# The opening of a two-block transformer kernel, with the first modulation made in two halves

## The chip, the cores and the metric

The kernel runs on one core of one Trainium2 chip. The metric is the device time of one execution in microseconds (us). The engines are TensorE (PE in the profile, its weight loads are PEld), VectorE (DVE), ScalarE (ACT), GpSimd (POOL) and SyncE (SP), which here only issues DMAs.

## The reference

Two blocks run one after the other on 256 tokens of width 1024, all in float32. The part that the opening computes is this:

```
cs  = silu(c)
mod = (cs @ ada_w[l] + ada_b[l]).reshape(3 sub-layers, [shift, scale, gate], 1024)
h   = rmsnorm(x, norm_g[l, 0]) * (1 + mod[0, scale]) + mod[0, shift]
x   = x + 0.5 * mod[0, gate] * (silu(h @ w_gate) * (h @ w_up)) @ w_down
...
(the same for a mixer of attention and convolution, and for a second FFN; two such layers;
 then a second block: FFN, a mixer of attention and a gated linear recurrence, FFN)
```

Before the first product with a weight of the FFN can start, `cs @ ada_w` must be known for the shift and the scale: two times 1024 columns of a matrix with 1024 rows, 8 MB in all.

## The kernel before

**Stages.** The program has nine stages (FFN, mixer, FFN, FFN, mixer, FFN, then FFN, mixer 2, FFN). Each reads its weights in units of 1 MB (128 partitions x 2048). SyncE loads a unit into one of three slots of `raw`, ScalarE rounds it to float32r into `hi` (`split`), VectorE subtracts to get the rest in `lo` (`split`, or `low_part` for half of a unit), and TensorE multiplies three times (`tok3`, `mm3`: high by low, low by high, high by high). The semaphores are `raw_full` (landed), `hi_done`, `lo_done` and `unit_done`. Unit n+3 takes the slot of unit n once its low part is made. Every engine works through its own instruction list strictly in the order in which the code is written; nothing is scheduled at run time, and semaphores alone tie the lists together.

**Tiles and chunks.** The 256 tokens are two tiles of 128. The 1024 columns of `x` are eight chunks of 128, which are turned by TensorE (`turn_x`) into PSUM (`PC`), scaled and shifted into `ub_b` and split into `nh` (high) and `nl` (low, by `lows`). ScalarE and VectorE do this in `apply`, pair of chunks by pair of chunks; `nh_done` and `nl_done` count the pairs.

**The opening.** The 8 MB of the first modulation come as eight units of 256 columns. Units 0 to 3 are the shift of chunks 0 to 7 (two chunks each), units 4 to 7 are the scale. VectorE makes five of them (0, 2, 4, 5, 7; `ada_unit`: one multiplication and seven multiply-adds over 128 x 256), and TensorE then sums each over the partitions with two products by a column of ones. TensorE makes the other three itself (`ada_cols_of`: 16 products of one column, each with a new weight of 128 x 128). Both write columns of `MOD` in PSUM. When all 16 columns are there (`mod_done`), `mods(0)` on VectorE makes `modt` (shift) and `nsc` (scale times gain), and `mods_rdy` lets `apply(0, 0)` start.

**The first FFN.** Its `up` products read two weight units: unit 0 holds the rows of chunks 0 to 3, unit 1 those of chunks 4 to 7 (`up(i, kh, t)`: group i, half kh, tile t; 12 products of 512 columns in `wide`). Group 0 is `up(0,0,0)`, `up(0,1,0)`, `up(0,0,1)`, `up(0,1,1)`. Then come the products of `bias_lines` and group 1.

**Two other places.** In the mixer of the first block twelve units make q and k (`unit_both`); VectorE adds their two halves (`qk_done`, one per unit), and `tick` starts the attention of one head and tile: logits on TensorE into the bank `SC`, bias and maximum on VectorE (`lg_done`), exponential on ScalarE. In the mixer of the second block `lru(3, 3)` makes the low part `cL` of the last two chunks of the recurrence, for which the product `yc` 0 waits at its chunk 6 (`first_recurrent`).

## Time and profile before

| | us |
|---|---|
| median of 3 runs | 2093.26 (2092.66 to 2093.48) |
| the profiled execution | 2095.6 |
| its span, first to last instruction | 2093.5 |
| PE busy in it | 2059.9 (98%) |
| DVE busy | 1432.5 (68%) |
| ACT busy | 1028.6 (49%) |
| DMA, mean over the span | 209 GB/s |

The profiled execution's own time is 2.1 us above its span, and 2.3 us above the median of the runs shown.

### The profile page before, as it was taken

The numbers are of one execution on the slowest core, as the hardware profiler recorded it, in microseconds if no ns is written. First come the engines' busy times: TensorE is split into PE (matmuls) and PEld (weight loads), VectorE is DVE, ScalarE is ACT, GpSimd is POOL, SyncE is SP. The second block draws the span as 40 slices with busy tenths as digits, with TensorE's granted clock in tenths as the row PEclk, the third lists the DMA queues.
The fourth block names the chain that finished last, engine by engine and source line by source line (L and its number), as shares of the span: only waits on it lengthen the run. The fifth ranks groups of instructions, "written<-read, shape, count | busy, mean of one in ns | idle before, by whom it ended". The sixth has DMA issues, their size and how long they took to land.

```text
span 2093.5 us, 28979 instructions
## 1 busy us (share of the span) xinstructions
PE 2059.9 (98%) x11649; PEld 1790.4 (86%) x11649; DVE 1432.5 (68%) x1822; ACT 1028.6 (49%) x1279; POOL 36.3 (2%) x78
## 2 busy tenths in 40 slices
PE   7999999999999999999999999999999999999998
PEld 7788888999888888888899998888788799998887
DVE  5887788668777677767866786455654669656454
ACT  4443544444554363445444445444644668646443
POOL 0000000000000000000000000000000010000000
PEclk9999999999999999999999999999999999999999
DMA  9787698447678748868865496654755454456652
GB/s 316 258 283 251 193 290 253 128 139 253 230 256 267 245 168 277 264 202 260 287 183 145 143 300 192 203 188 141 234 188 183 135 160 137 161 183 210 192 190 80
DMA packets 355929, 438.04 MB, mean 209 GB/s; under 512 B 9571, under 2 KB 323371, under 8 KB 355796
## 3 DMA queue, kind: packets, MB, share of 16 engines
q1 hardware_dynamic: 350592, 420.51, 61.7%
q0 software_dynamic: 4160, 14.23, 3.1%
q8 instruction: 92, 1.51, 0.3%
q10 hardware_dynamic: 1044, 1.46, 0.2%
q14 instruction: 41, 0.34, 0.0%
HBM read 435.05 MB, written 1.11 MB: 208 GB/s over the span
## 4 chain that ended last, share of the span: by engine, by line
PE 88%; DVE 5%; ACT 4%; issue 1%; DMA 1%; DVEq 1%; SPq 0%; ACTq 0%
PE PC L1808 7%; PE PC L1810 7%; PE PC L1809 7%; PE PA L1808 6%; PE PA L1810 6%; PE PA L1809 6%; PE PB L1808 6%; PE PB L1810 6%; PE PB L1809 6%; PE PA L1801 4%; PE PA L1802 4%; PE PA L1803 4%; PE PC L1839 3%; PE PC L1976 2%; PE PC L1801 2%; PE PC L1803 2%
## 5 line engine op out<-in xcount | busy, mean ns | idle before, releaser
L1172 DVE TENSOR_TENSOR lo<-raw,hi 128x2048 fp32r<-128x2048 f32 x274 | 626.7, 2289 | 209.5 <-ACT hi L696 208.4
L696 ACT ACTIVATE hi<-raw 128x2048 fp32r<-128x2048 f32 x277 | 529.3, 1912 | 260.1 <-PE PC L1810 114.8
L1198 DVE SCALAR_TENSOR_TENSOR acc<-raw,cs,acc 128x256 f32<-128x256 f32 x448 | 217.2, 485 | 34.4 <-issue 0.9
L1808 PE MATMUL PA<-hi,nn 128*128 128x512 f32 (+1 forms) x528 | 210.3, 398 | 7.0 <-DVE nn L1274 5.9
L1801 PE MATMUL PA<-nn,hi 128*128 128x256 f32 x720 | 209.0, 290 | 0.4 <-ACT f L1089 0.4
L1810 PE MATMUL PA<-hi,nn 128*128 128x512 f32 (+1 forms) x528 | 206.0, 390 | 0.0
L1809 PE MATMUL PA<-lo,nn 128*128 128x512 f32 (+1 forms) x528 | 205.5, 389 | 0.0
L1802 PE MATMUL PA<-nn,lo 128*128 128x256 f32 x720 | 203.6, 283 | 0.0
L1803 PE MATMUL PA<-nn,hi 128*128 128x256 f32 x720 | 203.6, 283 | 0.0
L1808 PE MATMUL PB<-hi,nn 128*128 128x512 f32 x400 | 158.2, 395 | 0.5 <-DVE nn L1274 0.5
L1810 PE MATMUL PB<-hi,nn 128*128 128x512 f32 x400 | 156.6, 391 | 0.0
L1809 PE MATMUL PB<-lo,nn 128*128 128x512 f32 x400 | 156.2, 391 | 0.0
L1172 DVE TENSOR_TENSOR w<-raw,w 128x2048 fp32r<-128x2048 f32 x51 | 116.8, 2289 | 50.4 <-ACT w L696 50.4
L1808 PE MATMUL PC<-hi,cL 128*128 128x512 f32 x384 | 151.1, 393 | 0.0
L1810 PE MATMUL PC<-hi,cH 128*128 128x512 f32 x384 | 149.6, 390 | 0.0
L1809 PE MATMUL PC<-lo,cH 128*128 128x512 f32 x384 | 149.5, 389 | 0.0
L1801 PEld LDWEIGHTS PA<-nn,hi 128*128 128x128 f32 x720 | 137.9, 192 | 1.9 <-issue 0.6
L1802 PEld LDWEIGHTS PA<-nn,lo 128*128 128x128 f32 x720 | 137.9, 192 | 0.1
L1803 PEld LDWEIGHTS PA<-nn,hi 128*128 128x128 f32 x720 | 137.8, 191 | 0.0
L1808 PEld LDWEIGHTS PA<-hi,nn 128*128 128x128 f32 x528 | 100.7, 191 | 30.4 <-issue 9.1
L696 ACT ACTIVATE w<-raw 128x2048 fp32r<-128x2048 f32 x51 | 97.5, 1911 | 48.0 <-PE PC L1810 44.1
L1810 PEld LDWEIGHTS PA<-hi,nn 128*128 128x128 f32 x528 | 100.6, 190 | 20.9
(317 smaller groups left out, 4088.8 us busy)
## 6 DMA issues: line engine op xcount, KB each, us to landing
raw<-in_w_in SPq DMA_DIRECT2D x90, 1024.0 KB, 5.4
raw<-in_ada_w SPq DMA_DIRECT2D x66, 1024.0 KB, 7.4
raw<-in_ffn_w_gate SPq DMA_DIRECT2D x88, 512.0 KB, 4.1
raw<-in_ffn_w_up SPq DMA_DIRECT2D x88, 512.0 KB, 5.2
raw<-in_ffn_w_down SPq DMA_DIRECT2D x44, 1024.0 KB, 5.2
raw<-in_ffn_w SPq DMA_DIRECT2D x88, 512.0 KB, 4.8
raw<-in_ffn_w SPq DMA_DIRECT2D x22, 1024.0 KB, 4.8
raw<-in_w_o SPq DMA_DIRECT2D x12, 1024.0 KB, 6.6
```

What stands on the lines that cost most here:

```text
L696: A(parts_of(n)[0], raw[:, n % 3, :], ACT.Copy).then_inc(hi_done, 1)
L1172: V.tensor_tensor(l, raw[:, n % 3, :], h.bitcast(F32), ALU.subtract).then_inc(lo_done, 1)
L1198: i = V.scalar_tensor_tensor(o, w[:, k, :], cs[:, k:k + 1], o, ALU.mult, ALU.add)
L1801: MM(o, wh[:, c0:c0 + w], xl, start=first, stop=False, skip_group_check=True)
L1802: MM(o, wl[:, c0:c0 + w], xh, start=False, stop=False, skip_group_check=True)
L1803: return MM(o, wh[:, c0:c0 + w], xh, start=False, stop=last, skip_group_check=True)
L1808: MM(o, xl, wh[:, c0:c0 + w], start=first, stop=False, skip_group_check=True)
L1809: MM(o, xh, wl[:, c0:c0 + w], start=False, stop=False, skip_group_check=True)
L1810: return MM(o, xh, wh[:, c0:c0 + w], start=False, stop=last, skip_group_check=True)
L1839: MM(o[:, m * 512:(m + 1) * 512].rearrange("p (e t) -> p e t", e=2), wh[:, c], nn[:, :, kk, :], start=kk == 0, stop=False, skip_group_chec ...
L1976: i = MM(SC[:, c0:c0 + w], qt[p0:p0 + HD, qc, (s % 2) * P:(s % 2 + 1) * P], kt[p0:p0 + HD, kc, 0:w], start=True, stop=True, skip_group_che ...
```

## The change

1. The eight units of the modulation are loaded in the order 0, 4, 1, 5, 2, 6, 3, 7: shift and scale of chunks 0 to 3 come first. The list of who makes which place stays (places 0, 2, 4, 5, 7 by VectorE, places 1, 3, 6 by TensorE). The FFN's weight unit 0 is loaded after the sixth place instead of after the eighth.
2. `mods(0)` becomes `half_mods(0)` and `half_mods(1)`, each for four chunks, with the semaphores `mod_first` and `half_rdy` for the first. ScalarE scales and shifts chunks 0 to 3 of both tiles, splits weight units 0 and 1 in between, and then does chunks 4 to 7 of both tiles; VectorE no longer scales any of tile 1.
3. TensorE's sums over partitions stand in a function of their own (`ada_sums(n)`, for the n-th of VectorE's places; it signals `mod_first` after the second and `mod_done` after the fifth). TensorE multiplies unit 0 with tile 0, then makes place 6 (`ada_cols_of(6)`), multiplies unit 0 with tile 1, sums the last unit, and then multiplies unit 1 with both tiles.
4. In the two mixers of the first block the first `tick` waits for 11 of the 12 additions of q and k, and the second for all 12.
5. In the second block's mixer VectorE does `lru(3, 3)` before `split(b + 19)` instead of after it.

```diff
+FIRST_ADA = (0, 4, 1, 5, 2, 6, 3, 7)
+def place(Aq, t, j):
+    if Aq == 0:
+        return 4 * (j // 2) + 2 * t + j % 2 + 1
+    return Aq * 8 + t * 4 + j + 1
...
@@ SyncE
-            for u in range(8):
-                sp.dma_start(first_ada(u), ada_v[0][:, :, u * UC:(u + 1) * UC])                    .then_inc(raw_full[u] if u < 4 else ada_in[u - 4], 16)
+            for u, c in enumerate(FIRST_ADA):
+                if u == 6:
+                    load(0, wg_v[0][:, 0:4, 0:UC], wu_v[0][:, 0:4, 0:UC])
+                sp.dma_start(first_ada(u), ada_v[0][:, :, c * UC:(c + 1) * UC])\
+                    .then_inc(raw_full[u] if u < 4 else ada_in[u - 4], 16)
...
@@ ScalarE
+            def first_apply(t, h):
+                act.wait_ge(tn_done, 2 * t + h + 1)
+                if t:
+                    act.wait_ge(nl_done, 4 * h + 2)
+                else:
+                    act.wait_ge(mods_rdy if h else half_rdy, 1)
+                for j in (2 * h, 2 * h + 1):
+                    for c in (2 * j, 2 * j + 1):
+                        i = A(ub_b[:, c, :], PC[:, t * D + c * P:t * D + (c + 1) * P], ACT.Identity,
+                              scale=nsc[:, c:c + 1], bias=modt[:, c:c + 1])
+                    i.then_inc(ua_done, 1)
+                    act.wait_ge(ua_done, place(0, t, j))
+                    A(nh[:, 2 * j:2 * j + 2, t * P:(t + 1) * P], ub_b[:, 2 * j:2 * j + 2, :], ACT.Copy)\
+                        .then_inc(nh_done, 1)
+            first_apply(0, 0)
             split(0)
-            apply(0, 0, lambda: split(1))
-            apply(0, 1)
+            first_apply(1, 0)
+            split(1)
+            first_apply(0, 1)
+            first_apply(1, 1)
...
@@ VectorE
+            def half_mods(h, done):
+                c = slice(4 * h, 4 * h + 4)
+                V.tensor_tensor(modt[:, :].rearrange("p (a k) -> p a k", a=2)[:, :, c],
+                                MOD.rearrange("p (a k) -> p a k", a=2)[:, :, c],
+                                vec[:, 0:16].rearrange("p (a k) -> p a k", a=2)[:, :, c], ALU.add)
+                dve.drain()
+                V.scalar_tensor_tensor(nsc[:, c], modt[:, 8 + 4 * h:12 + 4 * h], 1.0,
+                                       vec[:, V_NORM + 4 * h:V_NORM + 4 * h + 4], ALU.add, ALU.mult).then_inc(done, 1)
+                dve.drain()
...
                 if n == 3:
                     normed(0, 0)
+                    dve.wait_ge(mod_first, 1)
+                    half_mods(0, half_rdy)
+                if n == 4:
+                    lows(0, 0, (0, 1))
+                    low_part(0, 0)
+                    normed(0, 1)
+                    low_part(0, 1)
...
-            normed(0, 1)
-            mods(0)
-            low_part(0, 0)
-            lows(0, 0, (0,))
-            low_part(0, 1)
-            lows(0, 0, (1,))
+            lows(0, 1, (0, 1))
+            dve.wait_ge(mod_done, 1)
+            half_mods(1, mods_rdy)
             low_part(1, 0)
             lows(0, 0, (2,))
             low_part(1, 1)
             lows(0, 0, (3,))
-            dve.drain()
-            apply(0, 1)
+            lows(0, 1, (2, 3))
             split(2)
...
             def last_chunks():
+                lru(3, 3)
                 split(b + 19)
-                lru(3, 3)
...
@@ TensorE
-                up(0, 0, 0, s)
-                up(0, 1, 0, s, (lambda: turn_x(s, 1)) if s else None)
-                up(0, 0, 1, s)
+                if s:
+                    up(0, 0, 0, s)
+                    up(0, 1, 0, s, lambda: turn_x(s, 1))
+                    up(0, 0, 1, s)
+                else:
+                    up(0, 0, 0, s, lambda: turn_x(s, 1))
+                    ada_cols_of(6)
+                    up(0, 0, 1, s)
+                    ada_sums(4)
+                    up(0, 1, 0, s)
                 up(0, 1, 1, s)
...
+            ada_cols_of(1)
+            rows_turned()
+            ada_sums(0)
+            ada_cols_of(3)
+            ada_sums(1)
+            turn_x(0, 0)
+            pe.wait_ge(half_rdy, 1)
+            ada_sums(2)
+            ada_sums(3)
...
-                        if j == 0 and u == 0:
-                            pe.wait_ge(qk_done, 12 * (l + 1))
+                        if j == 0 and u < 2:
+                            pe.wait_ge(qk_done, 12 * l + 11 + u)
```

TensorE's list at the opening, before, from the first transpositions of tile 0 to the first six products of the FFN (`PB<-cs` is `ada_cols_of`, `PB<-ones` a sum over partitions, `PC<-ident` a transposition of `x`, `PA<-hi,nn` and `PA<-lo,nn` are products of the FFN):

```order
L1892 MATMUL PC<-ident,xn_b 128x128 x8
L2080 MATMUL PB<-cs,early 128x1 x16
L2095 MATMUL PB<-ones,acc 128x1 x4
L1892 MATMUL PC<-ident,xn_b 128x128 x8
L1808 MATMUL PA<-hi,nn 128x512
L1809 MATMUL PA<-lo,nn 128x512
L1810 MATMUL PA<-hi,nn 128x512
```

The same place in the changed kernel, where the lines of `kernel.py` have other numbers (six products stand in each gap marked by "..."):

```order
L1940 MATMUL PC<-ident,xn_b 128x128 x8
L2144 MATMUL PB<-ones,acc 128x1 x4
L1856 MATMUL PA<-hi,nn 128x512
...
L1940 MATMUL PC<-ident,xn_b 128x128 x8
L1856 MATMUL PA<-hi,nn 128x512
...
L2135 MATMUL PB<-cs,early 128x1 x16
L1856 MATMUL PA<-hi,nn 128x512
```

The 16 products of place 6, one sum and the transpositions of tile 1 have moved behind the first products of the FFN.

VectorE's list between the first normalized tile and the first low parts, before, with what each row waits for:

```order
L1234 RECIPROCAL rstd<-rowsq 128x1 [waits std_done]
L1249 TENSOR_SCALAR xn_b<-x,rstd 128x512 x2
L1195 TENSOR_SCALAR acc<-early,cs 128x256 [waits ada_in1]
L1198 SCALAR_TENSOR_TENSOR acc<-early,cs,acc 128x256 x7
L1195 TENSOR_SCALAR acc<-early,cs 128x256 [waits ada_in3]
...
L1216 TENSOR_TENSOR modt<-PB,vec 128x16 [waits mod_done]
L1219 SCALAR_TENSOR_TENSOR nsc<-modt,vec 128x8
L1179 TENSOR_TENSOR lo<-raw,hi 128x1024 [waits hi_done]
```

And in the changed kernel:

```order
L1571 TENSOR_TENSOR modt<-PB,vec 128x2x4 [waits mod_first]
L1575 SCALAR_TENSOR_TENSOR nsc<-modt,vec 128x4
L1229 TENSOR_SCALAR acc<-early,cs 128x256 [waits ada_in1]
L1232 SCALAR_TENSOR_TENSOR acc<-early,cs,acc 128x256 x7
L1308 TENSOR_TENSOR nn<-ub_b,nn 128x2x128 [waits nh_done] x2
L1213 TENSOR_TENSOR lo<-raw,hi 128x1024 [waits hi_done]
L1268 RECIPROCAL rstd<-rowsq 128x1 [waits std_done]
...
L1229 TENSOR_SCALAR acc<-early,cs 128x256 [waits ada_in3]
L1232 SCALAR_TENSOR_TENSOR acc<-early,cs,acc 128x256 x7
L1308 TENSOR_TENSOR nn<-ub_b,nn 128x2x128 [waits nh_done] x2
L1571 TENSOR_TENSOR modt<-PB,vec 128x2x4 [waits mod_done]
```

The low parts of tile 0's chunks 0 to 3 and of weight unit 0 now stand between the fourth and the fifth modulation unit; the second `modt` stands behind the fifth, and behind it unit 1's low part.

## Rows read from the trace of the kernel before

**Rows 1.** The page: engine, busy us, share of the span, instructions.
```profile
PE 2059.9 (98%) x11649; PEld 1790.4 (86%) x11649; DVE 1432.5 (68%) x1822; ACT 1028.6 (49%) x1279; POOL 36.3 (2%) x78
```

**Rows 2.** Timeline of PE: start us, us, line, operation; in brackets the idle time.
```profile
26.86 1.84 PE L2095 MATMUL PB<-ones,acc 128*128 128x1 f32 x8
28.57 1.95 PE L1892 MATMUL PC<-ident,xn_b 128*128 128x128 f32 x8
30.31 6.83 PE L2080 MATMUL PB<-cs,early 128*128 128x1 f32 x32
36.99 1.85 PE L2095 MATMUL PB<-ones,acc 128*128 128x1 f32 x8
38.70 1.95 PE L1892 MATMUL PC<-ident,xn_b 128*128 128x128 f32 x8
41.46 0.77 PE L1808 MATMUL PA<-hi,nn 128*128 128x512 f32 x1 [0.81 <-DVE nn L1274]
```

**Rows 3.** Timeline of DVE, the same stretch.
```profile
27.41 0.88 DVE L1249 TENSOR_SCALAR xn_b<-x,rstd 128x512 f32<-128x512 f32 x2
...
33.22 3.84 DVE L1198 SCALAR_TENSOR_TENSOR acc<-early,cs,acc 128x256 f32<-128x256 f32 x7
...
38.88 0.17 DVE L1216 TENSOR_TENSOR modt<-PB,vec 128x16 f32<-128x16 f32 x1 [0.79 <-PE PB L2095]
...
39.39 1.23 DVE L1179 TENSOR_TENSOR lo<-raw,hi 128x1024 fp32r<-128x1024 f32 x1
40.89 0.42 DVE L1274 TENSOR_TENSOR nn<-ub_b,nn 128x256 fp32r<-128x256 f32 x1 [0.28 <-ACT nn L767]
```

**Rows 4.** Timeline of ACT, the same stretch.
```profile
36.18 1.91 ACT L696 ACTIVATE hi<-raw 128x2048 fp32r<-128x2048 f32 x1 [8.02 <-DMA raw<-in_ffn_w_up]
39.40 1.15 ACT L761 ACTIVATE ub_b<-PC,modt,nsc 128x128 f32<-128x128 f32 x3 [1.31 <-DVE nsc L1219]
40.44 0.42 ACT L767 ACTIVATE nn<-ub_b 128x256 fp32r<-128x256 f32 x1
```

**Rows 5.** Windows: length, busy us (x) of PE, PEld, DVE, ACT, POOL, PEclk, DMA share, GB/s.
```profile
27.00:41.40 14.40, 13.65 (x65) 13.25 (x64) 11.56 (x28) 5.06 (x10) 0.00 (x0) 1.00 1.10 349
...
58.00:61.40 3.40, 3.40 (x10) 2.63 (x9) 3.40 (x6) 0.38 (x1) 0.00 (x0) 0.50 1.09 367
```

**Rows 6.** Timeline of PE from the end of group 0.
```profile
54.52 2.10 PE L2103 MATMUL PC<-oneh,relt 33*8 33x384 f32 x6
...
58.19 0.63 PE L1808 MATMUL PB<-hi,nn 128*128 128x512 f32 x1
58.62 0.63 PE L1809 MATMUL PB<-lo,nn 128*128 128x512 f32 x1
...
61.97 0.39 PE L1809 MATMUL PB<-lo,nn 128*128 128x512 f32 x1
62.20 0.39 PE L1810 MATMUL PB<-hi,nn 128*128 128x512 f32 x1
```

**Rows 7.** Timeline of PE at the sums of a later modulation.
```profile
227.30 0.95 PE L1869 MATMUL PB<-ones,acc 128*128 128x1 f32 x8
```

**Rows 8.** Timeline of PE and DVE at the first tick of the first mixer.
```profile
345.85 0.93 PE L1976 MATMUL PC<-k,q 64*128 64x128 f32 x6 [1.08 <-DVE k L1589]
...
349.78 1.56 PE L1976 MATMUL PC<-k,q 64*128 64x256 f32 x6
...
336.96 0.68 DVE L1589 TENSOR_TENSOR q<-PC,q 128x512 f32<-128x512 f32 x1
...
348.54 0.55 DVE L1462 TENSOR_REDUCE negm<-S 128x1 f32<-128x384 f32 x1
```

**Rows 9.** Timeline of PE and DVE at the recurrence's last chunk.
```profile
1811.62 0.39 PE L1801 MATMUL PA<-cL,hi 128*128 128x256 f32 x1 [1.23 <-DVE cL L1726]
...
1805.62 2.29 DVE L1172 TENSOR_TENSOR lo<-raw,hi 128x2048 fp32r<-128x2048 f32 x1 [1.13 <-ACT hi L696]
...
1810.88 0.68 DVE L1726 TENSOR_TENSOR cL<-acc,cH 128x512 fp32r<-128x512 f32 x1
```

More of the change, by code:

```diff
@@ L197, in squared @@
     return 3 * STAT[("p", s, t)] + (3 if h else 1)
+FIRST_ADA = (0, 4, 1, 5, 2, 6, 3, 7)
[3 more added lines that the diff above has]
+    return Aq * 8 + t * 4 + j + 1
 def by_act(Aq, t):
-    return 4 if t == 0 and Aq <= 7 else 2
+    return 4 if t == 0 and Aq <= 7 or Aq == 0 else 2
 def evicted(Aq, t, j):
@@ L1272, in lows @@
                 for j in pairs:
-                    dve.wait_ge(nh_done, Aq * 8 + t * 4 + j + 1)
+                    dve.wait_ge(nh_done, place(Aq, t, j))
                     V.tensor_tensor(nl[:, 2 * j:2 * j + 2, t * P:(t + 1) * P], ub[:, 2 * j:2 * j + 2, :],
@@ L1812, in need @@
             def need(Aq, t, k):
-                pe.wait_ge(nl_done, Aq * 8 + t * 4 + k // 2 + 1)
+                pe.wait_ge(nl_done, place(Aq, t, k // 2))
             def tile_of(v, k, t):
@@ L2079, in ada_cols_of, with ada_sums @@
                     for k in range(KC):
[L2080 removed]
+                        i = MM(MOD[:, m + f:m + f + 1], w[:, k, f * P:(f + 1) * P], cs[:, k:k + 1],
                                start=k == 0, stop=k == KC - 1, skip_group_check=True)
                 i.then_inc(ada_p, 1)
[L2084 to L2092 removed]
+            def ada_sums(n):
+                u = FIRST_ADA[(0, 2, 4, 5, 7)[n]]
                 pe.wait_ge(ada_d, n + 1)
@@ L2095, in _ @@
                     i = MM(MOD[:, c:c + 1], acc[:, c * P:(c + 1) * P], ones[:, 0:1], start=True, stop=True)
-            i.then_inc(mod_done, 1)
-            turn_x(0, 1)
+                if n == 1:
+                    i.then_inc(mod_first, 1)
+                if n == 4:
+                    i.then_inc(mod_done, 1)
+            ada_cols_of(1)
[7 more added lines that the diff above has]
+            ada_sums(3)
             def bias_lines():
```

18 lines of the change are left out of this document (5 added, 13 removed).

## The prediction

> **What bounds the kernel now.** I read the page's totals first: TensorE is busy for 98% of the span, VectorE for 68% [rows 1]. So an edit away from TensorE's list pays only where TensorE stands still, and an edit of its list pays only if it fills such a place or lets the same work run at the higher clock. Next I read TensorE's timeline over the opening, since that is where most of the edit lies. From 26.86 us it runs without a break through a sum, the transpositions of tile 0, the 16 products of place 6, another sum and the transpositions of tile 1; its first FFN product starts at 41.46 after 0.81 us of idle time [rows 2]. The window from 27 to 41.4 says the same: 13.65 of 14.40 us busy [rows 5]. The first thing to see is that in this stretch TensorE waits for neither the loads nor VectorE. It is the bound while it does the preparations themselves. Third, I read the pitch of the products. At 58 us two products of 512 columns stand 0.43 us apart and the granted clock is 0.50, the 1.2 GHz level; at 62 us they stand 0.23 us apart, at 2.4 GHz [rows 5, 6]. A sum's weight load takes 1.85/8 = 0.23 us in the opening [rows 2] and 0.95/8 = 0.12 us in the middle of the kernel [rows 7], and place 6 takes 6.83/32 = 0.21 us for each pass. So the preparations run at 1.2 GHz. The column PEclk is no guide there: it shows 1.00, and the pitch is what I go by. Last, I read VectorE and ScalarE over the same stretch [rows 3, 4], and both sides of the two small edits [rows 8, 9].
>
> **The opening, step by step.** Nothing is removed from TensorE's list: 48 products, place 6, five sums, two sets of transpositions, as before. What changes is when they can start, so I follow the new lists with the old durations. The sum that ends the first half is done at about 27.8 us, half of the pair that starts at 26.86 [rows 2]. VectorE ends the first normalization at 27.41 + 0.88 = 28.3, and `half_mods(0)` takes what `mods` took, from 38.88 to 39.39, 0.5 us [rows 3]: 28.8. Then comes its fourth unit. Seven of its eight instructions take 3.84 us [rows 3], all eight 4.3 us: 33.1. Two `lows` of 0.42 and half of unit 0's low part, 1.23 [rows 3], end at 35.2. ScalarE is in time for it: pair by pair it needs two evictions of 1.15/3 = 0.38 and a copy of 0.42 [rows 4], about 1.25 with the hand-over, so it starts at 28.9 with the first four transpositions and is through at 31.4. Weight unit 0 landed at 36.2 before [rows 4]; it now stands two units of 1 MB earlier in the queue, at 349 GB/s [rows 5] 3.0 us each, so at 30.2, and its high part (1.91 us) is there at 33.3. The loads behind it move by 3 us and cost nothing: place 6 and place 8 land by about 36, and are wanted at 42 and at 37.5.
>
> TensorE meanwhile has its transpositions of tile 0 (27.9 to 29.9), one sum (30.8), and then the other sum, which waits for the unit that ends at 33.1. **The first FFN product starts at 35.2 instead of 41.46.** TensorE has stood still for about 2.3 us before that sum and 1.2 us behind it; before, place 6 filled this time.
>
> From there on: six products at 0.43, 2.6 us (37.8); transpositions 1.95 (39.7); six products 2.6 (42.3); place 6, 6.83 (49.1). I take all of these at 1.2 GHz, since before they ran at that level, and the products among them come in bursts of 2.6 us with transpositions or one-column products between. Tile 1's chunks wait for nothing: VectorE ends the rest of unit 0 at 37.5, its fifth unit at 41.8 and two `lows` at 42.7. Then 12 products in a row. The low stretch from 58 to 61.4 held 3.4 us of back-to-back products before the clock rose [rows 5, 6], so I give them 3.4 us at 0.43 (8 products) and four at 0.23: 4.3 us (53.4). The last sum at the higher level takes 0.5 (53.9).
>
> Now the second half has to travel. Before, the last sum ended at 36.99 + 1.85 = 38.84 and the first product came at 41.46, 2.6 us later [rows 2], and 1.95 us of that were covered by the transpositions. Now nothing covers it. ScalarE has two evictions ahead of its copy where it had three, so I take 2.4 us: 56.3. Queued behind TensorE's wait is everything else; queued behind VectorE's wait for this sum is the low part of unit 1, which is made only afterwards. The last 24 products take 24 x 0.23 = 5.5 us, plus one stretch at the low level as at 58 us, 8 x 0.20 = 1.6 us, and 0.2 for the pairs that come one by one: 7.3 us. Group 0 ends at 63.6. Before it ended at 54.52 [rows 6]. **The opening costs 9.1 us.** The low stretch behind the bias products (2.10 us and more of small products) I leave as it was. Unit 2's low part follows ScalarE's table load and is ready while the bias products run, and later loads are ordered by low parts that shift along, with 5 us and more in hand; all that follows moves as one block.
>
> The count from the other side: TensorE's new idle times are 2.3, 1.2 and 2.4 us and some tenths, 6.1 in all, against 0.8 and 0.3 before, so +5.0 at an unchanged clock. The rest of the 9.1 is products run at 0.43 where they ran at 0.23.
>
> **Where the clock is uncertain** the same page of rows gives both bounds. With place 6 at the pitch of rows 7 it takes 32 x 0.12 = 3.8 instead of 6.83 us, 3.0 less. If the six products before it and all 36 behind it run at 0.23, that is 1.2 + 1.6 + 1.6 less, and the transpositions give 0.8; the waits for the single pairs then lie bare (0.7) and group 1 waits about 0.7 for unit 2. The opening then costs 9.1 - 8.2 + 1.4 = 2.3 us. At the other end all 36 products behind place 6 run at 0.43: 0.9 + 0.4 + 3.0 more, 13.4 us. I take the value between, because the two long bursts (12 and 24 products) are as long as those that raised the clock before, and the short ones are not.
>
> At 58 us the clock was low although TensorE had not stood still since its last wait, only done small products of the bias lines [rows 5, 6]. So I charge a low stretch behind the 2.4 us wait. The Trainium skill (TensorE: Matmul & The Clock Gate, "Why this matters for your kernels") asks only that TensorE has no long idle gap between bursts, and this wait is shorter than the gap that it names; by that rule the clock would stay high and the time would be 1.6 us less. The row speaks against relying on it.
>
> **The two small edits.** TensorE stood still for 1.08 us before the first `tick` for an addition that this tick does not read; the one it needs ended at 336.96 + 0.68, long before [rows 8]. With that wait gone, half a unit later TensorE meets the next one: VectorE's maximum comes at 348.54 + 0.55 = 349.1 whatever TensorE does, since VectorE is behind its own list, and the second tick started at 349.78. So 0.65 us are gained and not 1.08. Two layers: 1.3 (0 to 2.2). `lru(3, 3)`: TensorE stood still for 1.23 us for an operation that started at 1810.88, behind a `split`; the `split` ahead of both ends at 1805.62 + 2.29 = 1807.9, so the 0.68 us now end at 1808.6, before TensorE comes to it at 1810.3 [rows 9]. The `split` that it overtakes waits for ScalarE until about then anyway, and is wanted one unit (5.7 us) later. Gain 1.2 (1.0 to 1.4).
>
> **Sum.** 9.1 - 1.3 - 1.2 = +6.6 us. On the profiled execution's own time, 2095.6, that is 2102.2; it stands 2.3 above the median of the runs shown, so I say **2099.9**.
>
> **Rivals.**
> - *The clock rises early and stays*: high from 38 us on. For it: two of the bursts run into transpositions, not into idle time. Against: the same transpositions and place 6 ran low before for 14 us. Opening +2.3, in all -0.2: 2093.1.
> - *It rises for place 6 and falls again behind it.* 3.0 less for place 6 and 0.6 for some of the products around it: +3.0, 2096.3.
> - *It stays low through all of group 0*: opening +13.4, in all +10.9: 2104.2.
> - *Faster.* One mechanism: the clock is high from the very first product at 35.2, and the low stretch at 58 us falls away because the bias products now follow a long burst. On top of the first rival that saves 6 x 0.20 = 1.2, 1.6, and the whole 2.2 of the ticks instead of 1.3: -3.9. With the single pairs hidden too (0.7), -4.6: 2088.7. It decides only if TensorE is at 0.23 before 37.8 us and never falls back; one low stretch undoes it.
> - *The load order does nothing*, since TensorE never waited for these loads: true of the first product too, and part of my sum, not a case of its own.
>
> **How the numbers follow.** A measurement of this kernel tells 0.2%, 4.2 us, from no change. My forecast has 0.48, the wholly low clock 0.10, the middle case 0.20 (a fifth of it beyond 4.2 us), the early clock 0.16, the faster one 0.06. Slower by over 0.2%: 0.48 + 0.10 + 0.03 = 0.61; within: 0.33; faster: 0.06. The range leaves out the faster case, the lowest part of the early-clock one and most of the wholly low one: 2092.5 to 2103.5. The likeliest case alone spans 2098 to 2102.
>
> **What the changed profile would show.** Right: the first FFN product near 35.2, idle time of 2 and 1 us ahead of it, six products, transpositions, six products, place 6 of some 6.8 us from 42 to 49, an idle time of about 2.4 us near 54 ended by VectorE's `nn`, the bias products at about 63.6; the wait before the first tick gone, a few hundredths before the second, none for `cL`. Wrong: place 6 at 3.8 us, pitches of 0.23 from 38 us on, or bias products before 59. If the first product comes later than 36, VectorE's chain is longer than I read it.

## The result and the profile after

The changed kernel takes 2097.5 us (median of 20 runs, 2093.9 to 2099.93); the kernel before, run beside it, takes 2093.61 (20 runs, 2092.66 to 2096.6). The ratio is 1.0014, with a 95% interval of 1.0008 to 1.0019: slower by 2.9 us (1.7 to 4.0), or 3.9 by the medians. The profiled execution took 2096.57 us with a span of 2094.5, which answers to 2095.6 and 2093.5 before.

The page's totals answer to [rows 1]: TensorE is the bound as before, with 2 us less of busy time.

```profile
PE 2057.7 (98%) x11649; PEld 1788.1 (85%) x11649; DVE 1431.4 (68%) x1820; ACT 1030.4 (49%) x1283; POOL 36.5 (2%) x78
```

The timeline of TensorE over the opening, changed kernel (start us, us, line, operation; in brackets the idle time and what ended it). It answers to [rows 2] and [rows 6].

```profile
28.30 1.97 PE L1940 MATMUL PC<-ident,xn_b 128*128 128x128 f32 x8 [1.74 <-DVE xn_b L1283]
...
33.80 1.02 PE L2144 MATMUL PB<-ones,acc 128*128 128x1 f32 x4 [2.88 <-DVE acc L1232]
35.61 0.80 PE L1856 MATMUL PA<-hi,nn 128*128 128x512 f32 x1 [0.79 <-DVE lo L1213]
...
39.90 0.56 PE L1856 MATMUL PA<-hi,nn 128*128 128x512 f32 x1
40.29 0.39 PE L1857 MATMUL PA<-lo,nn 128*128 128x512 f32 x1
40.52 0.39 PE L1858 MATMUL PA<-hi,nn 128*128 128x512 f32 x1
...
41.43 3.63 PE L2135 MATMUL PB<-cs,early 128*128 128x1 f32 x32
...
47.78 0.50 PE L2144 MATMUL PB<-ones,acc 128*128 128x1 f32 x4
50.68 0.77 PE L1856 MATMUL PA<-hi,nn 128*128 128x512 f32 x1 [2.40 <-DVE nn L1308]
...
57.74 2.10 PE L2164 MATMUL PC<-oneh,relt 33*8 33x384 f32 x6
```

The first FFN product comes at 35.61 instead of 41.46, with the two idle times ahead of it. At about 40 us the distance between products of 512 columns falls from 0.43 to 0.23 us: the clock has risen. Place 6 (16 one-column products, which the profile counts as 32 passes) takes 3.63 us where it took 6.83. The wait for the second half is 2.40 us long. The bias products, which end group 0, come at 57.74 instead of 54.52: this execution loses 3.2 us in the opening.

The windows of the same stretch (length, busy us of PE, PEld, DVE, ACT and POOL, PEclk, DMA share, GB/s) show where the clock fell.

```profile
40.00:50.30 10.30, 8.28 (x56) 7.43 (x54) 4.10 (x10) 5.02 (x10) 0.69 (x1) 1.00 0.77 246
50.30:53.70 3.40, 3.02 (x7) 2.47 (x8) 2.02 (x4) 2.46 (x8) 0.00 (x0) 0.50 0.26 45
53.70:60.50 6.80, 6.80 (x26) 3.56 (x25) 3.18 (x4) 6.74 (x10) 0.00 (x0) 1.00 0.33 132
60.50:64.00 3.50, 3.50 (x9) 2.81 (x9) 3.50 (x4) 1.46 (x1) 0.00 (x0) 0.51 0.78 234
```

There is one stretch of 3.4 us at the 1.2 GHz level at the end of the 2.40 us wait, and one behind the bias products, which [rows 5] had too.

What the wait consists of stands in the timelines of VectorE and of ScalarE, changed kernel: VectorE adds the bias to the sum and makes the scale, ScalarE scales two chunks and copies them, VectorE makes the low half, and TensorE starts 0.14 us later.

```profile
48.32 0.17 DVE L1571 TENSOR_TENSOR modt<-PB,vec 128x8 f32<-128x8 f32 x1 [5.74 <-PE PB L2144]
...
50.11 0.43 DVE L1308 TENSOR_TENSOR nn<-ub_b,nn 128x256 fp32r<-128x256 f32 x1
```

```profile
48.82 0.81 ACT L1011 ACTIVATE ub_b<-PC,modt,nsc 128x128 f32<-128x128 f32 x2 [5.19 <-DVE nsc L1575]
49.66 0.42 ACT L1015 ACTIVATE nn<-ub_b 128x256 fp32r<-128x256 f32 x1
```

The small edits, in the timelines of TensorE at the second `tick` and of VectorE at `lru(3, 3)`: the answer to [rows 8] and [rows 9]. TensorE now waits 0.46 us for the maximum and no more for an addition, and the addition that makes `cL` stands ahead of the `split` of 2.29 us and not behind it; TensorE does not wait for it any more.

```profile
352.40 1.34 PE L2031 MATMUL PC<-k,q 64*128 64x256 f32 x5 [0.46 <-DVE negm L1496]
```

```profile
1810.25 0.69 DVE L1774 TENSOR_TENSOR cL<-acc,cH 128x512 fp32r<-128x512 f32 x1
1811.09 2.29 DVE L1206 TENSOR_TENSOR lo<-raw,hi 128x2048 fp32r<-128x2048 f32 x1 [0.15 <-ACT hi L711]
```

If the same products are matched in the two traces, the changed kernel stands 3.2 us later at 70 us, 2.6 behind the ticks of the first mixer, 2.9 ahead of those of the second and 2.2 behind them, 2.4 at 1800 us, and 0.9 behind the recurrence. So the ticks gave 0.6 us each, `lru` 1.5, and some tenths were lost on the way.

### The profile page after: what moved, and what is told of

It reads as the page before. It is cut to its first block, busy times and chain, and to the rows that moved or that the text cites. A ratio compares the mean times of both kernels' runs of the same rounds, so it can differ in the third digit from the quotient of the medians.

```text
span 2094.5 us, 28986 instructions
## 1 busy us (share of the span) xinstructions
PE 2057.7 (98%) x11649; PEld 1788.1 (85%) x11649; DVE 1431.4 (68%) x1820; ACT 1030.4 (49%) x1283; POOL 36.5 (2%) x78
## 4 chain that ended last, share of the span: by engine, by line
PE 86%; DVE 6%; ACT 4%; DMA 2%; issue 1%; DVEq 1%; SPq 0%; ACTq 0%
PE PC L1856 7%; PE PC L1858 6%; PE PC L1857 6%; PE PA L1856 6%; PE PA L1858 6%; PE PA L1857 6%; PE PB L1856 6%; PE PB L1858 6%; PE PB L1857 6%; PE PA L1849 4%; PE PA L1850 4%; PE PA L1851 4%; PE PC L1887 3%; DVE lo L1206 2%; PE PC L1849 2%; PE PC L2031 2%
```

## The experiments

Of each kernel the table gives the median of its runs with their number, the median of the kernel before, run beside it, and the ratio of the two with its 95% interval. The intervals are about 2 us wide to either side. Kernels with the same number in the column "before" were run side by side and compare more closely.

| kernel | us (lowest to highest, runs) | before | ratio | interval |
|---|---|---|---|---|
| opening_only | 2099.7 (2096.55 to 2103.17, 8) | 2093.95 | 1.0029 | 1.0018 to 1.0039 |
| small_edits | 2090.68 (2089.88 to 2091.65, 11) | 2093.95 | 0.9984 | 0.9975 to 0.9994 |
| clock_held | 2097.7 (2096.55 to 2102.03, 11) | 2093.95 | 1.0022 | 1.0013 to 1.0031 |
| place_six_early | 2096.21 (2094.43 to 2099.1, 11) | 2093.95 | 1.0011 | 1.0002 to 1.0020 |
| clock_held_wide | 2096.75 (2094.79 to 2101.18, 11) | 2093.39 | 1.0020 | 1.0011 to 1.0028 |
| wait_filled | 2094.96 (2093.8 to 2098.04, 11) | 2093.39 | 1.0009 | 1.0001 to 1.0018 |
| bias_spread | 2092.33 (2091.17 to 2093.95, 11) | 2093.39 | 0.9995 | 0.9986 to 1.0004 |
| opening_warm | 2102.02 (2101.12 to 2105.91, 5) | 2093.39 | 1.0044 | 1.0032 to 1.0057 |
| sum_first | 2092.55 (2090.65 to 2094.32, 11) | 2093.61 | 0.9994 | 0.9984 to 1.0003 |
| half_six_early | 2089.86 (2088.42 to 2091.19, 11) | 2093.61 | 0.9982 | 0.9973 to 0.9990 |
| half_six_again | 2089.98 (2088.62 to 2090.78, 11) | 2094.04 | 0.9977 | 0.9968 to 0.9986 |
| small_edits_again | 2091.12 (2089.91 to 2091.96, 11) | 2094.04 | 0.9986 | 0.9977 to 0.9994 |

### The two parts apart

`opening_only` is the changed kernel without the small edits:

```diff
-                lru(3, 3)
                 split(b + 19)
+                lru(3, 3)
...
-                        if j == 0 and u < 2:
-                            pe.wait_ge(qk_done, 12 * l + 11 + u)
+                        if j == 0 and u == 0:
+                            pe.wait_ge(qk_done, 12 * (l + 1))
```

> The changed kernel with the two small edits taken back, so the new opening alone. My theory: in every execution the new idle times (2.9, 0.8 and 2.4 us) are there, and the executions differ in when TensorE's clock rises: with it high through place 6 the opening costs about 3 us, with it low 6 to 9; so the times lie between 2096 and 2102 with a median near 2099.5 to 2100, in two groups, and wider apart than those of before. Rival: the spread comes from something else (loads that land at other times); then the opening's low stretches in the profile are those of the changed kernel's and the time is not tied to them.

`small_edits` is the kernel before with the same lines edited the other way, and nothing else.

> The kernel before with the two small edits alone (the first tick waits for 11 additions, lru(3, 3) stands before the split); the opening is the old one. My theory: they are worth 1.3 and 1.2 us as predicted, so 2.5 us or 0.12% less than before, the idle time for cL gone, and less than 0.1 us left before the second tick. First rival: a wait of about 0.5 us before each second tick takes the place of the one removed, and they give 2.0 us. Second rival: units further on wait longer and give it back; then the time is that of before.

The opening alone costs 6.1 us by its ratio (3.8 to 8.2), 5.75 by the medians; the small edits alone give 3.3 (1.3 to 5.2). The two ratios multiply to 1.0013, and the changed kernel has 1.0014: the parts add up, and the small edits cover half of what the opening costs. The runs of `opening_only` lie in two groups (2096.55 to 2097.96, and 2101.44 to 2103.17), as expected. Of the small edits one part was expected wrongly: not less than 0.1 but 0.46 us of idle time is left before the second tick, as in the changed kernel. This is what the first rival said, but the gain came out above its 2.0 us, and above the 2.5 of the theory.

The profiled execution of `opening_only` is one of the longer ones of its kernel (2101.44 us, span 2099.3); it shows what the changed kernel's profile was spared. Windows and timeline of TensorE:

```profile
40.40:43.80 3.40, 3.40 (x28) 3.21 (x27) 1.51 (x4) 2.62 (x4) 0.44 (x1) 1.00 1.10 348
43.80:50.70 6.90, 6.90 (x23) 5.84 (x23) 0.00 (x0) 0.00 (x0) 0.25 (x1) 0.51 0.52 175
50.70:54.10 3.40, 1.00 (x8) 0.86 (x7) 2.49 (x5) 2.16 (x6) 0.00 (x0) 1.00 0.00 0
54.10:57.50 3.40, 3.40 (x10) 2.62 (x9) 1.38 (x3) 2.46 (x7) 0.00 (x0) 0.50 0.45 130
```

```profile
41.32 4.51 PE L2135 MATMUL PB<-cs,early 128*128 128x1 f32 x32
...
53.74 0.47 PE L1856 MATMUL PA<-hi,nn 128*128 128x512 f32 x1 [2.40 <-DVE nn L1308]
...
60.97 2.10 PE L2164 MATMUL PC<-oneh,relt 33*8 33x384 f32 x6
```

Here the clock falls inside place 6 and stays low over the 12 products behind it (43.8 to 50.7), rises, and falls again at 54.1, 0.4 us after the end of the same 2.40 us wait. The bias products come 3.2 us later than in the changed kernel's profile, at the same program up to there: two stretches of 3.4 us more at the low level, 1.6 us each. A step of this kind may also be read in the runs of the changed kernel: its two runs with a mean granted clock of 0.998 took 2093.9 and 2094.2 us, the three with 0.995 from 2097.36 to 2099.93. A stretch of 3.4 us at half the clock takes 1.7/2094 = 0.0008 from the mean; 0.003 less is nearly four of them, and four times 1.6 us are the 6 us of the spread. That the spread is the number of such stretches in a run is an estimate and not seen run by run, since only one execution of each kernel has a trace. The mean clock does not order all the runs, either: those of the changed kernel with 0.996 lie between 2094.94 and 2098.72, and those of `opening_only` with 0.997 between 2096.55 and 2101.44.

### Holding the clock with extra products

`clock_held` puts products into TensorE's idle times whose results nobody reads: 24 and 6 of 128 columns around the fourth unit's sum, and 10 of 512 columns in the wait for the second half. The work of the reference is all still done.

```diff
+            fill(24)
             ada_sums(3)
+            fill(6)
...
                     ada_sums(4)
+                    fill(10, True)
                     up(0, 1, 0, s)
```

> The changed kernel with products that nobody reads put into TensorE's idle times: 24 of 128 columns while it waits for the fourth unit, 6 ahead of the first FFN product, 10 of 512 columns while the second half of the modulation travels. My theory (the clock makes the spread, and most of the loss is products at the low level): the first FFN products stand 0.23 us apart, no low stretch before the bias products, the times of all executions lie close together, at or below the fastest of the changed kernel, some 3 us below its median: 2093.5 to 2094.5. Rival (the idle times alone make the loss): the same median as the changed kernel's, 2097.5, since the idle times stay as long as they are.

Missed. The median, 2097.7, is the number of the rival, but not by its mechanism, since the idle times were filled. The 24 products took 5.36 us, twice the gap that they were to fill, at a pitch of 0.21 us for 128 columns, and pushed the first FFN product to 37.45. Timeline of TensorE:

```profile
30.16 5.36 PE L2146 MATMUL PB<-ones_w 128*128 128x128 f32 x24
```

The clock did not rise any earlier for them (40.5, against 40.1 in the changed kernel), and it was low from 47.3 to 50.7, in the 12 products. At the wait, which was filled, it did not fall.

`clock_held_wide` uses products of 512 columns instead: 6 and 1 before the first FFN product, one after every eighth pass of place 6, and 9 in the wait.

```diff
-                    ada_cols_of(6)
+                    ada_cols_of(6, 4)
...
                     ada_sums(4)
+                    fill(9)
...
+            pe.wait_ge(ones_rdy, 1)
+            fill(6)
             ada_sums(3)
+            fill(1)
```

> The changed kernel with products of 512 columns that nobody reads, this time fitted to the gaps: 6 in the 2.9 us wait for the fourth unit, 1 ahead of the first FFN product, one after each fourth product of place 6, 9 in the wait for the second half. The first try (clock_held) took products of 128 columns, whose pitch of 0.21 us made them overrun the gap by 2.4 us, and the clock did not rise under them. My theory (the clock makes the spread and the part of the loss above 2.5 us): place 6 takes 4.5 us with its four extra products in every execution, no low stretch between 38 us and the bias products, the executions lie within 2.5 us of each other and at the fastest of the changed kernel: median 2094 to 2095, some 3 us under it. Rival (the loss does not hang on the clock): 2097.5 or, with the extra products, more.

The clock now rose at 32.7 us, in front of the first FFN product, fell from 36.1 to 39.5, and stayed up through place 6, the 12 products and the filled wait to 60.0. Yet the theory missed: the median is 3.4 us above before, within 1 us of the changed kernel. The extra products in place 6 cost 0.9 us, and group 1 now waits 0.47 us for unit 2. It does so in all three kernels with the wait filled (0.46 to 0.48 us), because the 24 products behind the filled wait run without a low stretch and are done before unit 2's low part. Windows and timeline of TensorE:

```profile
32.70:36.10 3.40, 2.25 (x11) 1.46 (x10) 3.25 (x9) 0.51 (x1) 0.00 (x0) 1.00 1.10 349
36.10:39.50 3.40, 3.40 (x14) 2.93 (x13) 3.10 (x7) 1.31 (x4) 0.00 (x0) 0.50 1.09 350
...
43.00:60.00 17.00, 16.36 (x74) 10.95 (x73) 6.45 (x9) 10.14 (x18) 0.36 (x1) 1.00 0.45 150
60.00:63.40 3.40, 3.19 (x8) 2.51 (x9) 3.40 (x5) 1.97 (x2) 0.00 (x0) 0.50 0.55 164
```

```profile
60.21 0.80 PE L1856 MATMUL PB<-hi,nn 128*128 128x512 f32 x1 [0.47 <-DVE lo L1206]
```

Its spread stayed too (2094.79 to 2101.18), which the expectation had ruled out. The profile was its fastest run; what the slow ones do differently was not seen.

`wait_filled` fills only the wait, with 9 products of 512 columns.

```diff
                     ada_sums(4)
+                    pe.wait_ge(ones_rdy, 1)
+                    fill(9)
                     up(0, 1, 0, s)
```

> The changed kernel with 9 products of 512 columns that nobody reads in the 2.4 us wait for the second half of the modulation, and nothing else. My theory: the clock does not fall behind that wait (it fell at 50.3 us and stood low for 3.4 us in the changed kernel's profile), which is worth 1.4 us where it was high before; the spread by place 6 stays. Median 2096, still in two groups. Rival (what stands ahead of the wait, place 6 with its one-column products, makes the clock fall, and the wait only happens to follow): the low stretch is there all the same and the median is that of the changed kernel, 2097.5.

2094.96, under the expected 2096. By what each median stands above its own runs of before (1.6 against 3.9) that is 2.3 us under the changed kernel, by the ratios 1.0 us, and the intervals overlap. The lowest runs of the two kernels are the same, 2093.8 and 2093.9; what differs is how many of the runs lie near them. Its profile has the long low stretch of `opening_only` (44.6 to 51.4) and none at the wait:

```profile
44.60:51.40 6.80, 6.80 (x22) 5.64 (x22) 0.00 (x0) 0.00 (x0) 0.00 (x0) 0.50 0.38 136
51.40:66.00 14.60, 13.69 (x54) 8.52 (x55) 9.09 (x12) 12.12 (x19) 0.00 (x0) 1.00 0.28 89
```

That is now three kernels with the wait filled and no fall there, and three with the bare 2.40 us wait (changed kernel, `opening_only` and `place_six_early` below) and a low stretch at or just behind it, with one profiled execution of each.

### Place 6 in the idle time, whole

`place_six_early` moves `ada_cols_of(6)` ahead of the fourth unit's sum, where the old opening had it.

```diff
-                    ada_cols_of(6)
...
             ada_sums(2)
+            ada_cols_of(6)
             ada_sums(3)
```

> The changed kernel with place 6 moved back ahead of the first FFN product, into TensorE's idle time before the last sum of the first half. My theory: place 6 then always runs at 1.2 GHz, 6.8 us from its landing at 32.4 to 39.2, and the first FFN product starts at about 40 instead of 35.6; the end of group 0 comes 1 to 2 us later than in the changed kernel's profile, but the executions lie closer together, since the longest piece no longer depends on the level of the clock: 2097 to 2098, spread under 3 us. Rival (idle time alone counts): filling 3 us of idle time gives 3 us, 2094.5.

Timeline of TensorE:

```profile
31.99 6.99 PE L2134 MATMUL PB<-cs,early 128*128 128x1 f32 x32 [1.47 <-DMA early<-in_ada_w]
38.84 0.99 PE L2143 MATMUL PB<-ones,acc 128*128 128x1 f32 x4
39.70 0.77 PE L1856 MATMUL PA<-hi,nn 128*128 128x512 f32 x1
...
51.10 0.76 PE L1856 MATMUL PA<-hi,nn 128*128 128x512 f32 x1 [2.40 <-DVE nn L1308]
```

Before the first FFN product the clock is low, so place 6 costs 6.99 us again, waits 1.47 us for its load, and moves the first FFN product by 4.1 us; behind it that product's 3.6 to 4.5 us fall away. The balance is a gain of about 1 us that the intervals do not separate from the changed kernel. The median is under the expected 2097 to 2098, and the spread, 4.7 us, is above the expected 3: place 6 at a fixed length did not bring the executions together.

### The bias products, and the old opening with extra products

`bias_spread` is `small_edits` with the four bias products issued one by one between products of group 1, to spare the clock the block of small products that preceded the low stretch of [rows 6].

```diff
-                for g in range(3):
-                    MM(PC[0:8, g * 512:g * 512 + 384], relt1[:, g * 8:(g + 1) * 8], oneh1[:, g * 384:(g + 1) * 384],
-                       start=True, stop=True)
+                todo = iter(range(4))
+
+                def piece():
+                    g = next(todo)
...
-                    up(i, 0, 0)
+                    up(i, 0, 0, each=((1, 3), piece) if piece and i == 1 else None)
```

> The kernel before with the two small edits, and the four bias products no longer in one block behind group 0 but one by one between the products of group 1. My theory: the block of 2.8 us of small products is what makes the clock fall behind it in some executions (3.4 us low, 1.6 us lost); spread out they do not, so the median comes down by 0.5 to 1.6 us from that of small_edits, to 2089.1 to 2090.2, and the executions lie closer together. Rival: the fall comes from the stage ahead; no change, 2090.7.

Missed, 1.65 us slower than `small_edits` had been. The block had covered a wait. From the last product of group 0 to the end of group 1 this kernel takes 10.83 us, `small_edits` 8.70; the wait is 1.05 of the difference, and the rest goes to bias products that stand alone between products of 512 columns. Nor is the block by itself enough to make the clock fall: the profiles of both runs of the small edits have it (54.5 us) and no low stretch behind it. Timeline of TensorE at the first product of group 1:

```profile
55.53 0.47 PE L1808 MATMUL PB<-hi,nn 128*128 128x512 f32 x1 [1.05 <-DVE lo L1172]
```

`opening_warm` adds products of 512 columns to the whole old opening, on top of `bias_spread`: 14 at the start, and others between the passes of TensorE's three places and at the sums.

```diff
+            fill(14)
...
-                    ada_cols_of(1)
+                    ada_cols_of(1, 4)
+                    fill(6)
...
-                    ada_cols_of(3)
+                    fill(6)
+                    ada_cols_of(3, 2)
...
-                    ada_cols_of(6)
+                    ada_cols_of(6, 3)
```

> bias_spread's kernel with the old opening, and products of 512 columns that nobody reads in TensorE's idle times there (14 before place 1, 6 behind it, 6 ahead of place 3, 4 and 7 ahead of the third and the fifth sum, 3 ahead of the first FFN product) and between the products of places 1, 3 and 6; ScalarE makes the ones for them earlier. My theory: TensorE then runs the opening at 2.4 GHz, places 3 and 6 take about 5 us each instead of 6.8, the chain of VectorE becomes the bound, the last sum is done at 37.6 instead of 38.8 and the 7 first FFN products run at 0.23: 2.6 us less than bias_spread, 2087 to 2088. Rival 1: the clock does not rise under them, the extra products cost 0.43 each, and the time is 5 us or more above. Rival 2: it rises, but VectorE is the bound from the start and only the 1.4 us of the first products are gained: 2088.5.

The slowest of all, 2102.02, 9.7 us above `bias_spread`; of the three cases the first rival is the nearest, though the clock did rise. Windows:

```profile
10.20:13.60 3.40, 3.40 (x29) 3.24 (x28) 0.73 (x3) 0.00 (x0) 0.00 (x0) 1.00 1.10 339
13.60:20.40 6.80, 6.80 (x27) 5.92 (x26) 3.83 (x8) 0.00 (x0) 0.00 (x0) 0.50 1.07 351
20.40:27.20 6.80, 6.80 (x49) 6.25 (x47) 3.73 (x9) 6.41 (x16) 0.00 (x0) 1.00 1.10 351
27.20:44.30 17.10, 17.10 (x68) 15.65 (x67) 9.31 (x23) 3.71 (x5) 0.00 (x0) 0.50 0.99 315
```

The clock was up from 10.2 us and fell twice although TensorE was busy for every microsecond of these windows. One-column products with a product of 512 columns after every few of them did not hold it in place 1 and did not bring it back in place 6; in place 3 (20.4 to 27.2), and in place 6 of `clock_held_wide`, it stayed up.

### Hiding the trip of the second half

`sum_first` moves one line of the changed kernel, so that 12 products stand between the last sum and the first product that needs its result.

```diff
                     ada_cols_of(6)
-                    up(0, 0, 1, s)
                     ada_sums(4)
+                    up(0, 0, 1, s)
```

> The changed kernel with one step moved: the last sum of the modulation (four one-column products over acc, after the one-column products of the unit at place 6) is issued before the second up product of the first hidden chunk and not behind it. The 12 products of that up product took 2.8 us at the high clock in the changed kernel and stood before the sum; now they stand behind it, in the time in which the second tile's second half goes through the modulation, its normalization's last step and its split. Theory (the 2.40 us wait at 50.68 is the trip from the sum to the second half's operand, and it costs itself and the clock that falls to the low level behind it, 50.30 to 53.72): the wait is gone or under 0.3 us, the clock stays high from 40 to the bias products, group 1 starts 2.4 to 3.8 us earlier than at 60.52, and the median is 2093.3 to 2095, a ratio of 0.999 to 1.0007 to the kernel before. Rival (the wait moves and does not go): the 12 products wait themselves, for unit 1's low part or for the first hidden chunk's accumulator, or the second half comes no sooner because VectorE's split of unit 1 now stands behind the longer sum; then group 1 starts at 60 or later and the median stays within 0.7 us of the changed kernel's 2097.5.

The wait is gone: the view of TensorE's waits over the opening (engine, what, for whom: us, times, longest) has two left of the changed kernel's four, and the timeline runs from the sum to the bias products without a gap. (The other one that is missing is the 1.74 us before tile 0's transpositions, which cost nothing.)

```profile
PE PB L2144 <- DVE acc L1232: 2.9, 1, 2.9
PE PA L1856 <- DVE lo L1213: 0.8, 1, 0.8
```

```profile
45.77 0.99 PE L2144 MATMUL PB<-ones,acc 128*128 128x1 f32 x4
46.62 0.77 PE L1856 MATMUL PA<-hi,nn 128*128 128x512 f32 x1
...
56.85 2.10 PE L2164 MATMUL PC<-oneh,relt 33*8 33x384 f32 x6
...
59.63 0.50 PE L1856 MATMUL PB<-hi,nn 128*128 128x512 f32 x1
```

The median of 2092.55 is under the expected range. By the ratios, 1.0014 and 0.9994, the gain over the changed kernel is 4.2 us. The 2.40 of the wait and one low stretch of 1.6 would make 4.0; that split is worked out, not measured. But one part of the expectation failed in the profiled execution: the clock was low from 44.0 to 50.6, inside place 6 and the 12 products, as in `opening_only`, and group 1 started at 59.63, 0.9 and not 2.4 us earlier than in the changed kernel's profile, which had had no such stretch. From 50.6 to 64 us the clock was at 1.00 throughout.

`half_six_early` goes one step further: place 6 in two halves.

```diff
-                if u == 6:
+                if u == 7:
                     load(0, wg_v[0][:, 0:4, 0:UC], wu_v[0][:, 0:4, 0:UC])
...
-                    ada_cols_of(6)
+                    ada_cols_of(6, (1,))
...
+            ada_cols_of(6, (0,))
             ada_sums(3)
```

> The kernel of sum_first with one more move: the unit at place 6 is cut into its two halves of 16 one-column products. The first half stands in TensorE's idle time before the fourth unit's sum (2.88 us idle there in the changed kernel), the second stays behind the first up product; load 0, which reuses the load buffers in order, is issued one place later. Theory (idle time before the sum is free for work whose weights have landed at 32.35): 1.8 to 2.3 us of products leave the stretch behind the first up product; the fourth unit's sum is not later by more than 0.5 us (the first half may end at 35.4 at the low clock, 0.5 to 1.6 us behind the sum's place at 33.80, which is what the gain loses); group 1 starts 1 to 2 us earlier than in sum_first, and the median is 2091 to 2094. With the two small edits both in it, this kernel beats small_edits (2090.68) only if the opening as a whole has come out shorter than that of the kernel before. Rival (the first half delays the sum by what it takes): the sum and with it the first up product come 1.5 us or more later, VectorE and ScalarE shift with them, and the median is that of sum_first within 0.5 us or above it.

Timeline of TensorE:

```profile
30.20 3.55 PE L2135 MATMUL PB<-cs,early 128*128 128x1 f32 x16
33.61 0.99 PE L2145 MATMUL PB<-ones,acc 128*128 128x1 f32 x4
35.03 0.80 PE L1856 MATMUL PA<-hi,nn 128*128 128x512 f32 x1 [0.43 <-DVE lo L1213]
...
41.34 1.84 PE L2135 MATMUL PB<-cs,early 128*128 128x1 f32 x16
43.04 0.58 PE L2145 MATMUL PB<-ones,acc 128*128 128x1 f32 x4
...
53.43 2.10 PE L2166 MATMUL PC<-oneh,relt 33*8 33x384 f32 x6
...
56.21 0.50 PE L1856 MATMUL PB<-hi,nn 128*128 128x512 f32 x1
```

The first 16 passes (eight products; the unit has landed for them by 30.2 us, because weight unit 0 is now loaded behind it) run at the low clock, 3.55 us, and delay the sum by only 0.3 us against `sum_first`; behind the first FFN product 1.84 us are left of place 6. The bias products stand at 53.43, against 54.52 in [rows 6]: now the opening by halves is shorter than the old one. The median is 2.7 us less than that of `sum_first`, run side by side, and under the expected 2091 to 2094; group 1 starts 3.4 us earlier and not 1 to 2. The profile has one low stretch (44.0 to 47.4) where that of `sum_first` has two, so part of this may be the executions and not the edit.

Whether it also beats the small edits alone was tried with both run side by side:

> The kernel of half_six_early once more, this time on the same chip and in the same rounds as the kernel with the two small edits alone; the two differ only in the opening (old order against the order by halves, with the sum ahead of the second up product and the unit at place 6 cut in two). Theory A (the opening by halves in this order is shorter than the old one: the group of the second tile starts at 56.21 against 57.29 in the kernel before, and its clock falls once in the opening as it does there behind the bias products): this kernel is 0.5 to 1.5 us under small_edits_again, at 2089 to 2090.5. Theory B (the opening is worth nothing either way once its idle time is filled; the differences seen between calls, 2089.86 and 2090.68, are scatter): the two medians are within 0.4 us of each other.

> The kernel before with the two small edits alone, for a direct comparison with half_six_again in the same rounds. Theory A expects it 0.5 to 1.5 us above that kernel, theory B within 0.4 us of it. Both expect 2090.2 to 2091.2, a ratio of 0.998 to 0.9988 to the kernel before.

(What the expectation calls the group of the second tile is group 1.) The result is 2089.98 against 2091.12, with 10 of 11 and 3 of 11 runs under 2090.5: the opening by halves, in this order, gives 1.1 us by the medians (1.9 by the two ratios), and theory A holds. In this pair's profiles the bias products stand at 53.76 and 54.53. Both beat the kernel before and the changed one; the kernel of `half_six_early` and `half_six_again` is the fastest of the study, 4.8 us (2.9 to 6.7) under before in the second comparison.

## Why the prediction was right in sign and too high in size

Forecast were 2099.9 us and +6.6; measured are 2097.5 and +2.9 by the ratio.

- **The bound and the new starts: right.** The first FFN product was forecast at 35.2 and came at 35.61, the idle times at 2.3, 1.2 and 2.4 us and came at 2.88, 0.79 and 2.40. VectorE's chain decided them, and it ran at the durations of [rows 3]. The 1.74 us of idle time before tile 0's transpositions belong to the same chain and cost nothing, since the fourth unit's sum behind them waits anyway. No load was waited for in this stretch.
- **Place 6: the step that failed.** "Place 6, 6.83 (49.1). I take all of these at 1.2 GHz." The clock rose at about 40 us, in the second burst of six products, and place 6 took 3.63 us in the changed kernel and 4.51 in `opening_only`, 3.2 and 2.3 us less. The four products after the rise were at the high level, too. This is the rival "it rises for place 6 and falls again behind it", priced at +3.0, and it is nearly what came: the clock fell within place 6 in `opening_only`, and in the changed kernel's profile only behind the 12 products that follow. Two of the prediction's own signs of being wrong are there as well, place 6 under 3.8 us and bias products before 59. I had taken the low level from the old opening, in which no product of 512 columns stands before 41.46. Those bursts of six are what is new. `place_six_early`, which puts place 6 ahead of them again, has it at 6.99.
- **The opening: mis-sized term.** 9.1 us forecast, 6.1 measured in `opening_only`. The changed kernel's profile loses 3.2 us in the opening, 5.9 less than forecast: 3.4 in place 6, 0.9 ahead of it, 1.4 in the 12 products and 0.2 in the last 24. That of `opening_only` loses 6.45, 2.6 less: 2.4 in place 6 and 1.0 ahead of it, while the 12 products took 0.8 more.
- **The 12 products and the stretches.** I gave the 12 products one low stretch of 1.6. They took 2.9 us without one in the changed kernel's profile, had one in that of `clock_held`, and ran low from the first to the last or nearly so in `opening_only` and `wait_filled` (5.1 and 5.3 us). Right for some executions and not for others.
- **The 2.40 us wait and the low stretch charged behind it: right, and borne out by six profiles.** With the wait bare the clock was low at its end or 0.4 us behind it in three kernels of three; with the wait filled in none of three. In `sum_first`, where 12 products take its place, the clock stays up behind them (1.00 from 50.6 to 64 us). One execution of each kernel was profiled, and the clock also fell where TensorE had not stood still at all (in place 6 of `opening_only`, `wait_filled` and `sum_first`), so a wait is not the only thing that comes before a fall. The Trainium skill (TensorE: Matmul & The Clock Gate, "Why this matters for your kernels") warns, for drops in mid-kernel, only of long idle gaps between bursts. Here the fall came at a gap of 2.40 us, and at none, so by these runs its rule is not enough.
- **The small edits: somewhat low.** Forecast 1.3 for the ticks and 1.2 for `lru`. The trace gives 0.62 and 0.64 for the ticks, as worked out, and 1.5 for `lru`. The whole was 3.3 and 2.9 us in two comparisons, 2.5 forecast; the intervals hold both. The "few hundredths" of idle time before the second tick do not follow from the prediction's own sum: 1.08 less 0.65 leaves 0.43, and 0.46 was measured.
- **The chances.** They add up, but a fifth of 0.20 is 0.04 and not 0.03. By the ratio (+2.9) the change measured is that of the middle case (+3.0), which had a chance of 0.20. That the two agree to a tenth is luck, since the executions of the changed kernel differ by 6 us.
- **The faster rival did not come.** It needed a clock that is high from 35.2; no profile of the changed order without extra products showed that before 40. What did make this order faster was an edit of the kernel, the trip covered by work that was already on the list.

What stays open is why the clock falls within place 6 or the 12 products in some executions and not in others: extra products of 512 columns between the passes kept it up in the one profile taken of them, but the spread of that kernel's runs did not shrink.

## What to carry to other kernels

When an order is changed so that a late operand is split into halves, ask what stands between the second half's production and its first use: 12 products that were on the list anyway hid a trip of 2.4 us once they stood behind the sum instead of before it, and that one line was worth 4.2 us. Long work of small products can fill an idle time if it is cut to the size of the gap; whole it delays what the gap was waiting for. And price the clock for the new neighbours of an instruction, not for its old ones: the same 32 passes took 6.83 us behind other small work and 3.63 to 4.55 behind products of 512 columns.

## What the runs showed of the hardware

- In windows in which TensorE was busy for the whole time (`opening_warm`, 27.2 to 44.3 us), the granted clock was 0.50. It was doing one-column products, sums and transpositions then, with products of 512 columns between them, most of them single, and once four and once seven in a row.
- With 24 products of 128 columns in a row from 30.2 us on, at a pitch of 0.21 us, the clock rose only at 40.5 (`clock_held`); with 6 of 512 columns in the same place it rose at 32.7 (`clock_held_wide`), against 40.1 in the changed kernel.
- A low stretch of 3.4 us costs 1.6 us under products of 512 columns (8 of them at 0.43 instead of 0.23). Before the first rise of the clock the level is not in PEclk: from 36 to 40 us that column shows 1.00 while the products stand 0.43 us apart.
- The same program can have a different number of such stretches from one execution to the next; one profile of a kernel with this spread shows one of its cases only. The changed kernel's profile loses 3.2 us in the opening, that of `opening_only`, the same program there, 6.45.
